# Hybrid streaming encoder step with hierarchical MoE: group 0's expert inputs by one-hot products, and moved splits and first loads around it

## The chip, the core and the metric

The kernel runs on one core of one Trainium2 chip. The metric is the device time of one execution in microseconds, the median of the runs shown. The core has TensorE (PE, with its weight loads shown as PEld), VectorE (DVE), ScalarE (ACT), GpSimd (POOL), SyncE (SP, which here only issues DMAs) and 16 DMA engines. Each engine executes its own instructions in order, and they meet at semaphores.

## What is computed

One layer for two request groups, 256 prompt tokens and 64 sample tokens (320 rows of 1024 values): a mixer of three gated branches, and behind it a mixture of experts. Cut to what matters here:

```python
x = x + mixed @ p["w_out"]
x = x + hier_moe(rmsnorm(x, p["norm_moe_g"]), ...)

def hier_moe(x, w_rg, b_rg, w_re, b_re, w_g, w_u, w_d):
    p_group = softmax(xf @ w_rg + b_rg)
    p_top, grp = top_k(p_group, 1)                      # one of 4 groups
    e_in = (xf @ w_re + b_re) of that group             # 8 experts each
    top_vals, top_idx = top_k(e_in, 2)
    p_exp = softmax(top_vals) * p_top
    for e in range(32):
        hidden = silu(xf @ w_g[e]) * (xf @ w_u[e])      # 1024 -> 256
        y = y + combine[:, e:e + 1] * (hidden @ w_d[e]) # 256 -> 1024
```

Before the mixer's projections the memory rows are projected (w_mem_k, w_mem_v) after an RMSNorm of their own.

## The kernel before

**Precision.** A product of float32 values is made of three fast ones: each operand is split into a rounded high part (ScalarE, a Copy to float32r) and a rest (VectorE, x minus high), and TensorE multiplies high by high, high by rest and rest by high (`PARTS`). A weight unit of 1 MB (128 x 2048) is loaded by SP, its high part made by ScalarE, its rest by VectorE (L988 and L1378 for the dense stage, in a ring of two; L999 and L1387 for the experts, in eight slots). TensorE waits for the rest. Small matrices that need full precision are multiplied as plain float32.

**Order.** `make_steps` writes out a list of steps, and each engine's program walks it and takes from each step its own part. So the place of a step in the list sets the order on all engines. What an engine does besides is tied to a step: ROUND_AT says behind which residual steps (numbered 3 x quarter + place) ScalarE and VectorE split the expert units 0 to 4; LOGITS_AT behind which residual step a pair of logit blocks stands.

**The first microseconds.** SP loads the memory rows and unit 0 in halves, unit 1 and then the rows x, and unit 2 when unit 0's rest is made. At step "memnorm" ScalarE sums the squares of the memory rows (L995), takes the root and then makes unit 1's high part; VectorE computes the scale and then unit 1's rest. POOL loads two narrow slices of w_in (the gate weights, 16 bytes a row) at once.

**The residual stage.** For four quarters of w_out, TensorE makes the residual sums of three row tiles (128, 128 and 64 rows; steps "res": L680 for 128 rows, L606 for the samples, whose two parts lie side by side). VectorE adds them to x_tm (L1643, L1644), ScalarE squares them for the norm (L1200). Behind the first residual of a quarter's successor the previous quarter's columns are transposed (steps "hnT", L816), scaled by the norm's gain into hnT by ScalarE (even blocks, L1203) or VectorE (odd, L1649), and multiplied with the 36 router columns (steps "logits", L621, plain float32, summed over eight blocks). SP writes the finished rows to x_rows in HBM.

**Routing.** VectorE finds each token's group (one-hot `ohg`), TensorE counts each token's rank in its group (L820 to L822) and the totals (L825), VectorE makes `og` (L1347): for each group g a one-hot of tokens by slots (320 x 128). TensorE multiplies og with the token numbers (`slot_tokens`, L841), VectorE turns the result into row numbers (`slot_token`, `slot_out`), POOL gathers the rows of a group's tokens from x_rows (`gather_rows`, L1951), TensorE transposes them (`slot_rows_T`, L861: eight blocks, the columns taken with a step of eight), ScalarE makes the high part with the gain (`slot_x_high`, L1230, eight copies), VectorE the rest (`slot_x_rest`, L1371). Meanwhile VectorE works out the expert weights (from "totals", L1696, to `pone_r`, L1728), which TensorE turns into weights of slots (`slot_weights`, L873). Between these, `keep_busy` (L598) makes products whose results nobody reads.

**Experts.** 32 experts in four groups of eight. In program order on TensorE: gate and up of expert x, first half of the inner dimension (part "A", L896), then part "B", the transposition of the previous expert's hidden rows (L906) between them, and the previous expert's down product (L925). Each part reads one of the 96 units of `STREAM`.

```python
for x in range(E):
    gate_up(lv, x, "A")
    if x in WEIGHTS_AT: slot_weights(lv, WEIGHTS_AT[x])
    if x: hidden_T(lv, x - 1)
    gate_up(lv, x, "B")
    if x: down(lv, x - 1)
    if x in ROWS_AT: slot_rows_T(lv, ROWS_AT[x])
```

Should a group have more than 128 tokens, the whole expert stage is repeated as a further level, from code in a branch; with these inputs it is not.

## Time and profile before

| | |
|---|---|
| runs | 863.65, 863.71, 865.85 us; median 863.71 |
| profiled execution | 862.83 us, span of its instructions 861.0 us |
| TensorE busy | 838.0 us, 97% of the span |
| VectorE, ScalarE, GpSimd busy | 588.8, 471.5, 93.8 us (68%, 55%, 11%) |
| mean granted clock of TensorE | 0.988 of 2.4 GHz |
| HBM read, written | 178.55, 7.93 MB; 217 GB/s over the span |
| chain that ended last | L896 21%, L925 10% of the span, all others 1% or less |

In the rows below times are microseconds from the span's start. A timeline row gives start, duration, engine, line, operation, tiles, count, and in brackets how long the engine stood idle before it and what ended that. The duration of a merged row runs from the first start to the modelled end of the last; the spacing of two rows is read from their starts. Matmuls are pipelined, so a mean duration is longer than the spacing.

### The profile page before, as it was taken

How to read it: one execution, taken by the hardware profiler on the slowest of the kernel's cores; microseconds unless marked ns; L12 is line 12 of the kernel's file. 1: busy time of each engine (PE TensorE's matmuls, PEld its weight loads, DVE VectorE, ACT ScalarE, POOL GpSimd, SP SyncE). 2: the span in 40 equal slices, each digit the busy share in tenths (PEclk: the TensorE clock that was granted, in tenths of full speed). 3: DMA queues.
4: the chain of work that ended last, by engine and by line, in shares of the span. 5: the costliest groups of instructions: out<-in, count | busy, mean ns of one | idle time of the engine just before them, and what ended most of it. 6: DMA issues, size and time to landing. Idle time of an engine off the chain costs nothing. (4 is left out here: it accounts for less than half of the span.)

```text
span 861.0 us, 12938 instructions
## 1 busy us (share of the span) xinstructions
PE 838.0 (97%) x5133; PEld 762.6 (89%) x5133; DVE 588.8 (68%) x824; ACT 471.5 (55%) x639; POOL 93.8 (11%) x153
## 2 busy tenths in 40 slices
PE   6999999999999999999999999899999999999995
PEld 5999999999989998999999999788888888888883
DVE  5665487773445536786656457567889889899893
ACT  4665477753333234454333435545778677767763
POOL 3303001020011011000000000010003111310410
PEclk9999999999999999999999999979999999999998
DMA  8758533334344435345446454469999999999970
GB/s 268 220 169 282 188 111 111 111 123 138 110 135 135 146 123 172 107 139 167 140 147 220 146 197 148 171 223 356 362 341 365 367 388 386 355 375 362 377 270 18
DMA packets 100387, 186.61 MB, mean 217 GB/s; under 512 B 5668, under 2 KB 71488, under 8 KB 100320
## 3 DMA queue, kind: packets, MB, share of 16 engines
q1 hardware_dynamic: 95280, 171.47, 57.9%
q0 software_dynamic: 4240, 12.59, 4.4%
q10 hardware_dynamic: 800, 1.66, 0.5%
q8 instruction: 43, 0.70, 0.3%
q14 instruction: 24, 0.20, 0.1%
HBM read 178.55 MB, written 7.93 MB: 217 GB/s over the span
## 5 line engine op out<-in xcount | busy, mean ns | idle before, releaser
L1378 DVE TENSOR_TENSOR unit_r<-arena,unit_r 128x2048 fp32r<-128x2048 f32 x63 | 144.8, 2299 | 134.9 <-ACT unit_r L988 134.7
L1387 DVE TENSOR_TENSOR w_r<-arena,w_r 128x2048 fp32r<-128x2048 f32 x96 | 216.9, 2286 | 29.2 <-ACT w_r L999 29.2
L592 PE MATMUL pj<-xn_r,unit_r 128*128 128x320 f32 x1536 | 234.0, 311 | 0.0
L592 PEld LDWEIGHTS pj<-xn_r,unit_r 128*128 128x128 f32 x1536 | 225.5, 188 | 3.5 <-issue 3.0
L896 PE MATMUL pj<-w_r,xg 128*128 128x512 f32 x768 | 190.9, 398 | 0.2 <-ACT xg L1230 0.2
L999 ACT ACTIVATE w_r<-arena 128x2048 fp32r<-128x2048 f32 x96 | 180.3, 1909 | 4.4 <-DMA arena<-in_w_exp_up 4.4
L896 PEld LDWEIGHTS pj<-w_r,xg 128*128 128x128 f32 x768 | 141.8, 189 | 30.9 <-issue 0.3
L988 ACT ACTIVATE unit_r<-arena 128x2048 fp32r<-128x2048 f32 x63 | 120.1, 1907 | 24.6 <-PE pj L592 20.0
L925 PE MATMUL pj<-w_r,hidT 128*128 128x512 f32 x384 | 93.4, 392 | 0.6 <-ACT hidT L1243 0.6
L925 PEld LDWEIGHTS pj<-w_r,hidT 128*128 128x128 f32 x384 | 71.8, 188 | 17.1 <-issue 0.8
L592 PE MATMUL pj<-br_r,unit_r 128*128 128x320 f32 x384 | 59.6, 311 | 0.0
L592 PEld LDWEIGHTS pj<-br_r,unit_r 128*128 128x128 f32 x384 | 56.7, 188 | 1.1 <-issue 1.1
L662 PE MATMUL pj<-unit_r,mn_r 128*128 128x256 f32 x384 | 49.9, 291 | 1.8 <-DVE unit_r L1378 1.8
L1243 ACT ACTIVATE hidT<-ms 128x256 fp32r<-128x256 f32 x32 | 12.3, 385 | 71.8 <-PE ms L906 71.8
L662 PEld LDWEIGHTS pj<-unit_r,mn_r 128*128 128x128 f32 x384 | 48.3, 198 | 2.3 <-DVE unit_r L1378 1.8
L592 PE MATMUL pj<-unit_r,xn_r 128*128 128x256 f32 x384 | 48.4, 285 | 0.0
L592 PEld LDWEIGHTS pj<-unit_r,xn_r 128*128 128x128 f32 x384 | 46.7, 191 | 0.4 <-issue 0.3
L592 PE MATMUL pj<-u_r,unit_r 128*128 128x320 f32 x192 | 28.8, 309 | 0.0
L1137 ACT ACTIVATE arena<-pj 128x320 f32<-128x320 f32 x24 | 10.4, 433 | 33.3 <-PE pj L592 33.3
L592 PEld LDWEIGHTS pj<-u_r,unit_r 128*128 128x128 f32 x192 | 28.3, 188 | 0.0
L1394 DVE SCALAR_TENSOR_TENSOR arena<-arena,prT 128x323 f32<-128x323 f32 x48 | 26.9, 561 | 1.7
L680 PE MATMUL pj<-unit_r,mix_r 128*128 128x256 f32 x192 | 24.1, 283 | 0.1
(362 smaller groups left out, 813.3 us busy)
## 6 DMA issues: line engine op xcount, KB each, us to landing
arena<-in_w_in SPq DMA_DIRECT2D x40, 1024.0 KB, 5.2
arena<-in_w_exp_gate SPq DMA_DIRECT2D x64, 512.0 KB, 4.9
arena<-in_w_exp_up SPq DMA_DIRECT2D x64, 512.0 KB, 6.5
arena<-in_w_exp_down SPq DMA_DIRECT2D x64, 512.0 KB, 5.6
arena<-in_w_mem_v SPq DMA_DIRECT2D x4, 1024.0 KB, 6.8
arena<-in_w_br_mem SPq DMA_DIRECT2D x4, 1024.0 KB, 5.1
arena<-in_w_br_mlstm SPq DMA_DIRECT2D x4, 1024.0 KB, 5.1
arena<-in_w_br_gmlp SPq DMA_DIRECT2D x4, 1024.0 KB, 5.1
```

The costliest lines, as they stand in the source:

```text
L592: last = mm(bank_of(s)[0:out_rows, 0:out_cols], l, r, start=k == 0, stop=k == len(pairs) - 1)
L662: last = mm(b[:, 0:256], mn_r[:, p, k, a[1] * 128:a[1] * 128 + 128], w[:, q, k, :], start=k + m == 0, stop=k == KC - 1 and m == 2)
L680: last = mm(b[0:n, 0:256], mix_r[:, p, k, t0:t0 + n], w[:, q, k, :], start=k + m == 0, stop=k == KC - 1 and m == 2)
L896: last = mm(pj[:, x % 2, :].rearrange("p (h n) -> p h n", h=2), xg[g % 2][:, k0 + k, xp, :], w[:, wp, k, :, :], start=k0 + j == 0, stop=k0 ...
L925: last = mm(pj[:, 2 + half, :], hidT[:, x % 2, xp, c, :], w_r[u % NS][:, wp, c * D + half * 512:c * D + half * 512 + 512], start=e == 0 an ...
L988: af(unit_r[n % RING][:, 0, :], ringw[:, n % RING, :], ACT.Copy).then_inc(u_hi, 1)
L999: af(w_r[u % NS][:, 0, :], raw_w[u % NS], ACT.Copy).then_inc(m_hi, 1)
L1137: af(sg[:, k % 2, :], b[:, 0:T], ACT.Sigmoid).then_inc(free, 1)
L1243: af(hidT[:, x % 2, 0, :, :].rearrange("p a b -> p (a b)"), ms[:, x % 2, 0:DE], ACT.Copy).then_inc(m_hth, 1)
L1378: v.tensor_tensor(unit_r[n % RING][:, 1, :], ringw[:, n % RING, :], unit_r[n % RING][:, 0, :], ALU.subtract).then_inc(u_lo, 1)
L1387: v.tensor_tensor(w_r[u % NS][:, 1, :], raw_w[u % NS], w_r[u % NS][:, 0, :], ALU.subtract).then_inc(m_lo, 1)
L1394: ins = v.scalar_tensor_tensor(o, r[:, j:j + CONVW], prT[:, P_CW + 16 * j + c:P_CW + 16 * j + c + 1], o, ALU.mult, ALU.add)
```

## The change

1. *First loads.* POOL issues the two loads of the gate weights only when unit 1 has landed. At "memnorm" ScalarE and VectorE split unit 1 before they work on the memory rows' norm.
2. *Residual stage.* The logits of blocks 2 and 3 stand behind the sample tile of the last quarter, block 4 behind the last residual, block 5 behind the last transpositions. VectorE makes the rests of expert units 2 and 3 behind hnT 3 and hnT 5 instead of behind residual steps.
3. *Group 0's inputs.* TensorE makes the transposed rows of group 0's slots directly, as x_tm (as weights, with a step of eight) times group 0's one-hot, 24 plain float32 products over three row tiles (`first_rows_T`), in place of eight transpositions of gathered rows. The products with token numbers stand behind expert 0's two halves (`first_tokens`), the row numbers are made behind the first hidden rows (`first_index`), so all gathers come later; group 0's gathered rows are used only for its residual sum. The keep-busy products behind "totals" and before the first rows are gone.
4. *Order on ScalarE and VectorE.* ScalarE copies the first four blocks before the router's Exp, the other four behind it, then splits units 6 and 7. VectorE makes the first four rests before its work of "totals", the other four behind pone_r, and the level counters behind those.

The diff, cut to its core:

```diff
@@ -55,13 +55,14 @@
 ROUND_AT = {1: 0, 5: 1, 6: 2, 8: 3, 10: 4}
+REST_AT = {1: 0, 5: 1, 10: 4}
 NO_ROW = 512
...
 QK0, V0, O0, I0, F0, U0, GV0, MQ0, GATE0 = 0, 2048, 3072, 4096, 4100, 4104, 5128, 6152, 7176
-LOGITS_AT = {(2, 0): 1, (2, 2): 2, (3, 1): 3}
+LOGITS_AT = {(2, 0): (0, 1), (3, 0): (2, 3), (3, 2): (4,)}
 RES_ORDER = ((0, 1, 2), (0, 1, 2), (0, 1, 2), (2, 0, 1))
@@ -188,12 +189,12 @@
                     step("hnT", c, ring="hx", eng="AD"[c % 2])
-            if (u, j) in LOGITS_AT:
-                for c in (2 * LOGITS_AT[u, j] - 2, 2 * LOGITS_AT[u, j] - 1):
-                    step("logits", c, ring=None, eng=None)
+            for c in LOGITS_AT.get((u, j), ()):
+                step("logits", c, ring=None, eng=None)
     step("moe_var", ring=None, eng=None)
...
     step("hnT", 7, ring="hx", eng="D")
+    step("logits", 5, ring=None, eng=None)
     step("moe_norm", ring=None, eng=None)
@@ -824,16 +825,12 @@
                 last.then_inc(ready[s["ring"]], 1)
-                if kind == "totals":
-                    keep_busy(2)
             def slot_tokens(lv):
-                until(pe, m_xgl, 2 * G * lv)
-                if isinstance(lv, int):
-                    pe.wait_ge(s_tokid, 1)
+                pe.wait_ge(m_xgl, 2 * G * lv)
                 for g in range(G):
@@ -842,6 +839,23 @@
                         last.then_inc(m_slot, 1)
+            def first_tokens(g0, g1):
+                for g in range(g0, g1):
+                    for i in range(3):
+                        last = mm(ms[:, 3, 2 * g:2 * g + 2], og[:, i, g, :], tokid[:, i, :], start=i == 0, stop=i == 2)
+                last.then_inc(m_slot, 1)
+            def first_rows_T():
+                pe.wait_ge(m_onehot, 1)
+                for half in range(2):
+                    for k in range(4):
+                        for i, (t0, n) in enumerate(TILES):
+                            cols_of = x_tm[0:n, i, :].rearrange("t (p k) -> t k p", k=KC)
+                            last = mm(pj[:, 2 + half, k * 128:(k + 1) * 128], cols_of[:, 4 * half + k, :], og[0:n, i, 0, :].bitcast(FP32), start=i == 0, stop=i == 2)
+                    last.then_inc(m_rowT, 1)
             def slot_rows_T(lv, g):
@@ -851,6 +865,7 @@
                         pe.wait_ge(freed["hx", e], _seen["hx", e])
+                    pe.wait_ge(m_outrow, 2 * lv + 2)
                 if g >= 2:
@@ -880,7 +895,7 @@
                     k0 = 4
-                if x == 0 and part == "A":
+                if x == 0 and part == "A" and not isinstance(lv, int):
                     pe.wait_ge(m_index, 2 * lv + 2)
@@ -929,18 +944,25 @@
             def level(lv):
-                slot_tokens(lv)
                 if isinstance(lv, int):
-                    keep_busy(9)
-                slot_rows_T(lv, 0)
+                    first_rows_T()
+                else:
+                    slot_tokens(lv)
+                    slot_rows_T(lv, 0)
                 for x in range(E):
...
                         slot_weights(lv, WEIGHTS_AT[x])
+                    if x == 0 and isinstance(lv, int):
+                        pe.wait_ge(s_tokid, 1)
+                        pe.wait_ge(m_onehot, G)
+                        first_tokens(0, 2)
                     if x:
...
                     gate_up(lv, x, "B")
+                    if x == 0 and isinstance(lv, int):
+                        first_tokens(2, G)
                     if x:
@@ -1015,12 +1044,12 @@
                 if kind == "memnorm":
+                    unit_first_part(1)
                     for i in range(2):
...
                     af(sd[:, 3:5], var[:, 3:5], ACT.Sqrt).then_inc(s_sd, 1)
-                    unit_first_part(1)
                 elif kind == "xnorm":
@@ -1206,9 +1235,12 @@
                 elif kind == "lgt":
                     unit_high(0, 5)
-                    unit_high(0, 6)
+                    act.wait_ge(s_gpk, 16)
+                    slot_x_high(0, 0, 0)
                     act.wait_ge(s_lgx, 1)
                     af(expo.rearrange("p a b -> p (a b)"), expo.rearrange("p a b -> p (a b)"), ACT.Exp).then_inc(s_lge, 1)
+                    slot_x_high(0, 0, 1)
+                    unit_high(0, 6)
                     unit_high(0, 7)
...
                 if kind == "unit_split":
@@ -1407,11 +1436,11 @@
                 if kind == "memnorm":
+                    unit_second_part(1)
                     dve.wait_ge(s_ss, 2)
...
                     refine(1, 3, 5, s_rsm)
-                    unit_second_part(1)
                 elif kind == "xnorm":
@@ -1642,11 +1671,13 @@
                     v.tensor_tensor(x_, x_, b[0:n, 0:256], ALU.add).then_inc(free, 1)
-                    if 3 * u + s["place"] in ROUND_AT:
-                        unit_rest(0, ROUND_AT[3 * u + s["place"]])
+                    if 3 * u + s["place"] in REST_AT:
+                        unit_rest(0, REST_AT[3 * u + s["place"]])
                 elif kind == "hnT" and a[0] % 2:
...
                     v.tensor_scalar(hnT[:, c, :], b[:, 0:T], prT[:, P_MOE + c:P_MOE + c + 1], None, ALU.mult).then_inc(free, 1)
+                    if c in (3, 5):
+                        unit_rest(0, 2 if c == 3 else 3)
                 elif kind == "moe_var":
@@ -1676,9 +1707,7 @@
                     dve.wait_ge(*done("ranks"))
-                    token_onehots(0, 2)
-                    slot_index(0, 0)
-                    token_onehots(2, G)
+                    token_onehots(0, G)
                     v.tensor_tensor(expo[:, :, 0:G], lg[:, :, 0:G], gmax[:, :, 0:1].to_broadcast([128, 3, G]), ALU.subtract)
@@ -1690,16 +1719,11 @@
                     v.tensor_tensor(expo[:, :, G:G + 1], emax[:, :, 1:2], emax[:, :, 0:1], ALU.subtract).then_inc(s_lgx, 1)
-                    slot_index(0, 1)
-                    output_rows()
+                    dve.wait_ge(s_gpk, 16)
+                    slot_x_rest(0, 0, 0)
                 elif kind == "totals":
...
                     v.tensor_copy(cnt[:, 3:4], cnt[:, 0:1]).then_inc(free, 1)
-                    link(v.tensor_scalar(cnt[:, 1:2], cnt[:, 0:1], SLOTS + 0.5, None, ALU.is_ge))
-                    for lv in range(2, LEVELS):
-                        link(v.tensor_scalar(cnt[:, 2:3], cnt[:, 0:1], lv * SLOTS + 0.5, None, ALU.is_ge))
-                        link(v.tensor_tensor(cnt[:, 1:2], cnt[:, 1:2], cnt[:, 2:3], ALU.add))
-                    v.tensor_copy(more[:, :], cnt[:, 1:2]).then_inc(s_more, 1)
                     for i in range(3):
@@ -1726,6 +1750,12 @@
                     v.tensor_tensor(pone_r[:, 1, :, :], weights, pone_r[:, 0, :, :], ALU.subtract).then_inc(s_pone, 1)
+                    slot_x_rest(0, 0, 1)
+                    link(v.tensor_scalar(cnt[:, 1:2], cnt[:, 0:1], SLOTS + 0.5, None, ALU.is_ge))
+                    for lv in range(2, LEVELS):
+                        link(v.tensor_scalar(cnt[:, 2:3], cnt[:, 0:1], lv * SLOTS + 0.5, None, ALU.is_ge))
+                        link(v.tensor_tensor(cnt[:, 1:2], cnt[:, 1:2], cnt[:, 2:3], ALU.add))
+                    v.tensor_copy(more[:, :], cnt[:, 1:2]).then_inc(s_more, 1)
                 if kind == "unit_split":
@@ -1754,19 +1784,25 @@
             def y_add(lv, g, half):
...
                     dve.wait_ge(m_yhalf, G * lv + g + 1)
+                    if g == 0 and isinstance(lv, int):
+                        dve.wait_ge(m_row[0], 16)
                 else:
...
             def level(lv):
-                slot_x_rest(lv, 0)
+                if not isinstance(lv, int):
+                    for half in range(2):
+                        slot_x_rest(lv, 0, half)
                 for u in (range(5, 6) if isinstance(lv, int) else range(2, 5)):
...
                     hidden(lv, x - 1)
+                    if x == 1 and isinstance(lv, int):
+                        first_index()
                     if x > 1 and x - 1 in WEIGHTS_AT:
@@ -1855,6 +1892,7 @@
             pool.wait_ge(s_wifz, 1)
+            pool.wait_ge(unit_full[1], 16)
             for c0, col in ((0, I0), (32, F0)):
...
```

TensorE in the last quarter of the residual stage, before. The first L606 group is the sample tile of quarter 2, the second that of quarter 3 (`pair_mix`, 16 products); L621 are logits (three tiles a block, `wr` the router columns); L816 hnT 4 and 5; L680 a tile of 128 rows.

```order
L606 MATMUL pj<-unit_r_53,pair_mix 128x256 x16
L621 MATMUL ms<-wr,arena 128x36 x2
L621 MATMUL ms<-wr,arena 64x36
L621 MATMUL ms<-wr,arena 128x36 x2
L621 MATMUL ms<-wr,arena 64x36
L606 MATMUL pj<-unit_r_54,pair_mix 128x256 x16
L816 MATMUL ms<-ident,arena 128x128 x2
L816 MATMUL ms<-ident,arena 128x64
L816 MATMUL ms<-ident,arena 128x128 x2
L816 MATMUL ms<-ident,arena 128x64
L680 MATMUL pj<-unit_r_54,mix_r 128x256 x24
```

The same place with the change (L607, L622, L817, L681 are the same lines, shifted).

```order
L607 MATMUL pj<-unit_r_53,pair_mix 128x256 x16
L607 MATMUL pj<-unit_r_54,pair_mix 128x256 x16
L817 MATMUL ms<-ident,arena 128x128 x2
L817 MATMUL ms<-ident,arena 128x64
L817 MATMUL ms<-ident,arena 128x128 x2
L817 MATMUL ms<-ident,arena 128x64
L622 MATMUL ms<-wr,arena 128x36 x2
L622 MATMUL ms<-wr,arena 64x36
L622 MATMUL ms<-wr,arena 128x36 x2
L622 MATMUL ms<-wr,arena 64x36
L681 MATMUL pj<-unit_r_54,mix_r 128x256 x48
```

The logits of blocks 2 and 3 stood between the two sample groups; they stand now behind the transpositions, and the sample groups follow each other.

VectorE there, before: L1644 and L1643 add a residual tile (64 rows: samples), L1649 is hnT 3, L1387 the rest of an expert unit (`w_r_62` unit 2, `w_r_63` unit 3).

```order
L1644 TENSOR_TENSOR arena<-arena,pj 128x256
L1387 TENSOR_TENSOR w_r_62<-arena,w_r_62 128x2048
L1658 MEMSET arena 64x36
L1659 MEMSET arena 128x15
L1661 CAST tokid<-tokf 128x6
L1644 TENSOR_TENSOR arena<-arena,pj 128x256
L1649 TENSOR_SCALAR arena<-ms,prT 128x320
L1643 TENSOR_TENSOR arena<-arena,pj 64x256
L1644 TENSOR_TENSOR arena<-arena,pj 64x256
L1387 TENSOR_TENSOR w_r_63<-arena,w_r_63 128x2048
L1643 TENSOR_TENSOR arena<-arena,pj 64x256
```

With the change (L1673, L1672, L1678, L1416):

```order
L1673 TENSOR_TENSOR arena<-arena,pj 128x256
L1689 MEMSET arena 64x36
L1690 MEMSET arena 128x15
L1692 CAST tokid<-tokf 128x6
L1673 TENSOR_TENSOR arena<-arena,pj 128x256
L1678 TENSOR_SCALAR arena<-ms,prT 128x320
L1416 TENSOR_TENSOR w_r_62<-arena,w_r_62 128x2048
L1672 TENSOR_TENSOR arena<-arena,pj 64x256
L1673 TENSOR_TENSOR arena<-arena,pj 64x256
L1672 TENSOR_TENSOR arena<-arena,pj 64x256
L1673 TENSOR_TENSOR arena<-arena,pj 64x256
L1678 TENSOR_SCALAR arena<-ms,prT 128x320
```

Unit 2's rest stood ahead of the addition of the second tile and stands behind hnT 3; unit 3's stood ahead of the sample tile of quarter 3 and now comes behind hnT 5.

TensorE from the totals (L825) to expert 0's second half, before. L598 are keep-busy products, L841 products with token numbers, L861 the transpositions, L896 gate and up, L873 slot weights.

```order
L825 MATMUL ms<-arena,ones 128x4 x3
L598 MATMUL pj<-ident 128x128 x2
L841 MATMUL ms<-tokid,og 128x2 x3
L841 MATMUL pj<-tokid,og 128x2 x9
L598 MATMUL pj<-ident 128x128 x9
L861 MATMUL pj<-ident,arena 128x128 x8
L896 MATMUL pj<-w_r_60,xg_69 128x512 x12
L873 MATMUL ms<-pone_r,og 128x20 x3
L896 MATMUL pj<-w_r_61,xg_69 128x512 x12
```

With the change (totals L826, L856 the new products, L911 gate and up, L888 slot weights, L846 token numbers):

```order
L826 MATMUL ms<-arena,ones 128x4 x3
L856 MATMUL pj<-og,arena 128x128 x24
L911 MATMUL pj<-w_r_60,xg_69 128x512 x12
L888 MATMUL ms<-pone_r,og 128x20 x3
L846 MATMUL ms<-tokid,og 128x2 x6
L911 MATMUL pj<-w_r_61,xg_69 128x512 x12
L846 MATMUL ms<-tokid,og 128x2 x6
L911 MATMUL pj<-w_r_62,xg_69 128x512 x12
```

Two groups of keep-busy products, the token products and the transpositions between the totals and expert 0 are replaced by 24 products of the residual rows with `og`; the token products stand on both sides of expert 0's second half.

## Rows read from the trace of the kernel before

**Rows 1.** Groups of TensorE's instructions; columns: busy us, mean ns, idle before.

```profile
L896 PE MATMUL pj<-w_r,xg 128*128 128x512 f32 x768 | 190.9, 398 | 0.2 <-ACT xg L1230 0.2
...
L598 PE MATMUL pj<-ident 128*128 128x128 f32 x30 | 6.2, 379 | 0.0
```

**Rows 2.** Timeline of the first 60 us, SP, ScalarE and TensorE.

```profile
3.71 0.66 SPq L557 DMA_DIRECT2D arena<-in_w_mem_k  x1
...
15.48 1.90 ACT L988 ACTIVATE unit_r<-arena 128x2048 fp32r<-128x2048 f32 x1
...
19.76 3.13 PE L662 MATMUL pj<-unit_r,mn_r 128*128 128x256 f32 x24 [1.57 <-DVE unit_r L1378]
...
21.91 1.92 ACT L988 ACTIVATE unit_r<-arena 128x2048 fp32r<-128x2048 f32 x1 [3.21 <-DMA arena<-in_w_mem_k]
...
26.30 3.11 PE L662 MATMUL pj<-unit_r,mn_r 128*128 128x256 f32 x24 [0.24 <-DVE unit_r L1378]
```

**Rows 3.** DMA issues from 3.7 to 4.1 us; columns: count, KB each, us to landing.

```profile
arena<-in_w_mem_k SPq DMA_DIRECT2D x1, 1024.0 KB, 11.0
```

**Rows 4.** Timeline of the residual stage, TensorE and one row of VectorE.

```profile
538.13 2.28 DVE L1387 TENSOR_TENSOR w_r<-arena,w_r 128x2048 fp32r<-128x2048 f32 x1
...
538.25 2.18 PE L606 MATMUL pj<-unit_r,pair_mix 128*128 128x256 f32 x16
...
542.22 1.97 PE L621 MATMUL ms<-wr,arena 128*128 128x36 f32 x12 [1.80 <-ACT arena L1203]
...
544.12 3.33 PE L606 MATMUL pj<-unit_r,pair_mix 128*128 128x256 f32 x16
...
558.04 1.67 PE L621 MATMUL ms<-wr,arena 128*128 128x36 f32 x12 [0.70 <-ACT arena L1203]
...
559.64 1.40 PE L598 MATMUL pj<-ident 128*128 128x128 f32 x8
```

**Rows 5.** Windows of TensorE; columns: us, busy (instructions), granted clock, DMA share, GB/s.

```profile
543.00:544.00 1.00, 1.00 (x8) 0.67 0.99 393
546.00:547.00 1.00, 1.00 (x7) 0.63 0.00 0
560.00:561.00 1.00, 1.00 (x8) 0.70 0.89 332
570.00:571.00 1.00, 1.00 (x8) 0.68 0.66 217
```

**Rows 6.** Timeline of routing and the first experts, TensorE.

```profile
562.86 1.42 PE L825 MATMUL ms<-arena,ones 128*128 128x4 f32 x6
...
564.14 1.20 PE L598 MATMUL pj<-ident 128*128 128x128 f32 x4
...
567.79 3.61 PE L598 MATMUL pj<-ident 128*128 128x128 f32 x18
...
571.24 1.13 PE L861 MATMUL pj<-ident,arena 128*128 128x128 f32 x8
...
572.53 3.13 PE L896 MATMUL pj<-w_r,xg 128*128 128x512 f32 x12 [0.16 <-ACT xg L1230]
...
575.49 0.40 PE L873 MATMUL ms<-pone_r,og 128*128 128x20 f32 x3
...
575.74 5.83 PE L896 MATMUL pj<-w_r,xg 128*128 128x512 f32 x24
...
581.41 0.38 PE L906 MATMUL ms<-ident,arena 128*128 128x128 f32 x2
```

**Rows 7.** Timeline of routing, ScalarE and VectorE.

```profile
568.30 0.14 DVE L1696 TENSOR_REDUCE cnt<-ms 1x1 f32<-1x4 f32 x1
...
572.02 2.17 ACT L1230 ACTIVATE xg<-pj,gpk 128x128 fp32r<-128x128 f32 x8 [0.27 <-PE pj L861]
...
573.04 0.28 DVE L1728 TENSOR_TENSOR pone_r<-arena,pone_r 128x120 fp32r<-128x120 f32 x1
...
573.27 2.16 DVE L1371 SCALAR_TENSOR_TENSOR xg<-pj,gpk,xg 128x128 fp32r<-128x128 f32 x8
```

More of the change, by code:

```diff
@@ L992, in first_unit_high, with slot_x_high @@
                 af(unit_r[0][:, 0, cs], ringw[:, 0, cs], ACT.Copy).then_inc(signal, 1)
+            def slot_x_high(lv, g, half):
+                banks = pj if g == 0 else ms
+                act.wait_ge(m_rowT, 2 * (G * lv + g) + half + 1)
+                for j in range(4):
+                    k = 4 * half + j
+                    af(xg[g % 2][:, k, 0, :], banks[:, 2 + half, j * SLOTS:(j + 1) * SLOTS], ACT.Copy, scale=gpk[:, k:k + 1]).then_inc(m_xgh, 1)
             def memory_squares(i):
@@ L1271, in level @@
                     if x - 1 in ROWS_AT:
-                        slot_x_high(lv, ROWS_AT[x - 1])
+                        g_next = ROWS_AT[x - 1]
+                        if g_next >= 2:
+                            act.wait_ge(m_used, NU * lv + AT[EPG * (g_next - 1) - 1, "B"] + 1)
+                        for half in range(2):
+                            slot_x_high(lv, g_next, half)
                     hidden_high(lv, x - 1)
@@ L1762, in level @@
             def level(lv):
-                slot_x_rest(lv, 0)
+                if not isinstance(lv, int):
+                    for half in range(2):
+                        slot_x_rest(lv, 0, half)
                 for u in (range(5, 6) if isinstance(lv, int) else range(2, 5)):
@@ L1783, in level @@
                     if x - 1 in ROWS_AT:
-                        slot_x_rest(lv, ROWS_AT[x - 1])
+                        for half in range(2):
+                            slot_x_rest(lv, ROWS_AT[x - 1], half)
                     hidden_rest(lv, x - 1)
```

35 lines of the change are left out of this document (13 added, 22 removed).

## The prediction, made before the run

> **What bounds the kernel now.** I read the grouped instruction lines of TensorE first. The reader is to see there that in the expert stage 768 products of w_r and xg wait 0.2 us in all [rows 1]: from the first expert on TensorE sets the pace, and every microsecond by which the experts start earlier is one by which the kernel ends earlier. The timelines then show where TensorE waits for others, and that is at two places, the ones that the change touches.
>
> At the start [rows 2] TensorE stands 1.57 us before unit 1 (at 19.76) for VectorE's split, which follows ScalarE's first part at 15.48, and 0.24 us before unit 2 (at 26.30). In the residual and router stage [rows 4] it stands 1.80 us before the logits of blocks 2 and 3 and 0.70 us before those of 6 and 7. The windows of the granted clock [rows 5] show the rest: the clock falls from 2.4 to 1.2 GHz at 543.3, after the first of these waits and products of 36 columns, is back at 546.7, falls again at 560.4 after the second, and is back at 570.6. Both returns come about 2.7 us after a dense run of products began (544.12 [rows 4], 567.79 [rows 6]).
>
> I measure everything to one point, the transposition of expert 0's hidden rows (L906, 581.41 [rows 6]): what follows it is the same in both kernels and is TensorE's own work.
>
> **Start: 0.2 us.** Unit 1 was issued at 3.71 and took 11.0 us to land [rows 2, 3], so it lies there at 14.7, and ScalarE began on it at 15.48 because of two sums of squares. Moved ahead of them it gains 0.8 us for unit 1, and the squares still fit before unit 2. But unit 2 is then what TensorE waits for: ScalarE stood 3.21 us for its data until 21.91 [rows 2], and the split and the products follow from there. The wait before 19.76 shrinks and the one before 26.30 grows by as much. Unit 2 comes earlier only if the gate weights, whose loads POOL now issues behind unit 1, had been in its way; they are 32 KB, but in small pieces. Bounds: nothing, and both waits, 1.8 us. I take 0.2, nearest to the row in which data, not an engine, is late.
>
> **Residual stage: 4.1 us.** The logits of 2 and 3 move behind the sample rows of the last quarter and its two transpositions; block 4 goes to the end of the residuals, 5 behind the last transpositions. VectorE's rest of unit 2, 2.28 us at 538.13 [rows 4], moves behind the third and fourth transposed block, so the additions and hnT 3 come some 2 us earlier; the rest of unit 3 moves likewise. Both units are read by TensorE only in expert 1, behind expert 0's two halves, from about 578 on (575.74 + 2.96 [rows 6]), so their cover is ample. TensorE from 538.25: two sample groups of 2.1 (the row's 2.18 less its tail), 0.3 of waiting for VectorE's addition, transpositions 1.1, two logit blocks 1.5, two dense groups of 24 in 5.9 together, logits 0.8, transpositions 1.15, three logit blocks of 0.8: 17.3 us, so the logits end at 555.55 and not at 559.64 [rows 4]. Read by what vanishes: 1.8 and 0.7 of waiting, 1.15 of the sample group at the low clock (3.33 against 2.18), 0.4 in other waits and slower logits. Bounds 3.2 (if the clock is low in the last logits already) and 4.4. The copy of x_rows and the loads of units 6 and 7 are issued earlier with it; ScalarE reaches unit 6 only after group 0's eight copies, but TensorE reads it in expert 2, behind the point that I measure to, so nobody waits.
>
> **Routing: 1.1 us given back.** From the end of the logits to the first keep-busy product after the totals are 4.5 us (559.64 to 564.14 [rows 4, 6]); group 0's one-hot is there by then. Removed on this path: 22 keep-busy instructions, 12 token products, the gather and eight transpositions. Added are 24 fp32 products of 128 columns, 48 instructions, since an fp32 product takes two (12 logit instructions for six products). Their price is in no row as such. At the high clock 12 logit instructions with the same alternation of 128- and 64-row tiles start 1.60 us before what follows, 0.133 each [rows 4]; at the low one six take 1.28 us, 0.213 each [rows 6]. So all 48 cost between 6.4 and 10.2 us. The clock is most likely low when they begin, since the 8 us before hold logits, short products and waits as before 560.4. I take it back to 2.4 GHz after 2.8 us, as both returns in rows 5: 13 instructions at 0.213, 35 at 0.133, 7.45 us.
>
> Now both paths, counted from 560.05 (555.55 + 4.5). TensorE: products to 567.5, the first gate and up half 2.96 us (572.53 to 575.49 [rows 6]), to 570.5. The router weights: the first 24 instructions end at 564.3 (2.8 + 11 x 0.133); ScalarE's four copies start 0.27 later and take half of 2.17; VectorE's four rests 0.1 later half of 2.16; then VectorE's chain from the totals to pone_r, from 568.30 to 573.32, less four one-element counters now moved behind, 0.15 each by their like at 568.30, 4.4 [rows 7]. Sum 7.0, so pone_r is ready at 571.3. This is the **new wait**: the chain was done 2.2 us before TensorE asked (573.32 against 575.49) and now comes 0.85 late, because the four rests stand ahead of it on VectorE and they wait for ScalarE. From 571.35: slot weights 0.25, six token products, the second half 2.96, six token products, expert 1's first half 2.8. The token products I take at 0.55 for six (three router products of rows 6 start 0.25 before the next; all at the low clock they would be 1.3). That gives 578.45 against 581.41, **2.95 us** earlier; 4.1 won before, 1.1 given back.
>
> The work behind keeps its cover. After pone_r VectorE does xg's second half (1.1), the counters (0.6), the rest of unit 5 (2.3) and the comb copies (0.4), 4.4 us; only then can the first activation and hidden product run, and TensorE asks for them 7.1 us after pone_r. The slot numbers and the gathers come some 9 us later; TensorE needs their rows first in expert 5 and VectorE at the end of group 0. SP's next load (unit 8) waits for the first half's end, which is earlier than before.
>
> **Sum.** 2.9 + 0.2 = 3.1 us. The profiled execution spans 861.0 and took 862.83; it becomes 857.9 and 859.7. The median of the three runs, 863.71, lies 0.9 over the profiled one, so I forecast **860.6**. A measurement of this kernel can tell about 0.3% (2.6 us) from no change.
>
> **Rivals.**
> 1. *The products run slowly throughout*: the clock stays low to their end, 10.2 us. Half at 565.15, pone_r at 572.15, first gate half ended at 573.2, the point at 580.4: 1.0 gained and 0.2 at the start, 862.5. For: the clock stayed low for 10 us (560.4 to 570.6) in spite of the keep-busy and token products in it. Against: two returns after 2.7 us. 0.15.
> 2. *The residual stage keeps its wait*: what held hnT was VectorE's queue, and the later place lets another of its tasks (unit 3's rest, the additions) stand in the way for the same 1.8 us. 862.4. Against: with the rests moved VectorE is free when the samples' products end. 0.10.
> 3. *The start pays in full*: the gate weights were the delay, unit 2 lands up to 1.6 us sooner and both waits go. Then 3.1 + 1.6, 859.0. For: ScalarE, VectorE and TensorE are all free to use it. Against: the data before unit 2 are the same in sum. 0.15.
> 4. *Slower: dear products.* The residual rows are read as weights with a step of eight elements. If such a load does not hide behind the product before it, an instruction costs the 0.379 us that a keep-busy product has by itself [rows 1]: 18.2 us, the point at 588.4, 7.0 later, less 0.2: 870.5. It decides from 11.25 us on, 0.234 an instruction. Against: eight transpositions with the same step are done in 1.13 us [rows 6], 0.14 each, tail included. 0.05.
>
> On rival 4 the Trainium skill has a rule: *SBUF — State Buffer*, section "Door 1: The DMA port swizzle", in the note on cachelines, says that a read with a step over four fp32 elements pays for every new line, and this step is eight. By that rule the products would go the way of rival 4; the transposition row does not agree with it, and I leave the sum as it is.
>
> The forecast itself has 0.55, with a range of its own from 859.5 to 861.9. **Faster** by over 0.3% (under 861.1): rival 3 and four fifths of the forecast's own, 0.59. **Within**: rivals 1 and 2 and the rest, 0.36. **Slower**: rival 4, 0.05. The range reaches from rival 3 with the clock high in all products (858.0) to rival 1 with the residual stage at its lower bound of 3.2 (863.3).
>
> **What would show it.** The logits should follow without a wait before 543; their last instruction should end near 555.5 and the clock not fall before about 553. The products are 48 instructions starting near 560, in 6.4 to 10.2 us; in that time the clock rises. Then a wait of about 0.9 us before the slot weights, released by VectorE's pone_r, and the L906 of expert 0 near 578.3. At the start the wait before unit 1 falls to about 0.8 and that before unit 2 grows to about 1. I am wrong if an instruction of the products costs over 0.2 us at the high clock, if the wait for pone_r is over 2 us, or if TensorE still waits a microsecond or more among the residual groups.

## Result and the profile after

The changed kernel takes 871.33 us (median of four runs, 869.92 to 872.14) against 864.35 (863.65 to 865.85) for the kernel before: ratio 1.0079, 95% interval 1.0063 to 1.0094, **slower** by 7.0 us (0.8%). The forecast was 860.6 with a range from 858.0 to 863.3. The profiled execution spans 868.2 us and took 869.92.

Timeline of TensorE in the changed kernel, the start and the stretch from the last residual quarter to the point (rows give start, duration, line, operation):

```profile
core 0 of [0], span 868.2 us
...
10.44 10.89 PE L663 MATMUL pj<-unit_r,mn_r 128*128 128x256 f32 x72
...
26.14 1.07 PE L663 MATMUL pj<-unit_r,mn_r 128*128 128x256 f32 x7 [1.64 <-DVE unit_r L1407]
...
538.07 4.10 PE L607 MATMUL pj<-unit_r,pair_mix 128*128 128x256 f32 x32
...
552.37 2.93 PE L622 MATMUL ms<-wr,arena 128*128 128x36 f32 x18
555.23 2.08 PE L599 MATMUL pj<-ident 128*128 128x128 f32 x8
...
559.73 16.24 PE L856 MATMUL pj<-og,arena 128*128 128x128 f32 x48
575.90 5.45 PE L911 MATMUL pj<-w_r,xg 128*128 128x512 f32 x12
581.19 0.40 PE L888 MATMUL ms<-pone_r,og 128*128 128x20 f32 x3
...
588.44 0.38 PE L921 MATMUL ms<-ident,arena 128*128 128x128 f32 x2
```

Read beside [rows 2, 4, 6]: no wait stands in the residual stage any more, and the logits end at 555.23 where they ended at 559.64. The products (L856, 48 instructions) begin at 559.73 and last until the first gate half starts at 575.90: 16.17 us. That half takes 5.29 us to 581.19 and not 2.96. Then no wait for pone_r, and the point, the transposition of expert 0 (now L921), stands at 588.44 and not at 581.41: 7.03 later. The spans differ by 7.2, so nothing that matters happens behind it.

The windows of the changed kernel (columns as in [rows 5]; the number after POOL's busy time is the granted clock, 0.50 for 1.2 GHz and 1.00 for 2.4):

```profile
553.00:554.00 1.00, 1.00 (x9) 0.87 (x8) 0.86 (x6) 1.00 (x1) 0.00 (x0) 0.94 0.98 234
554.00:555.00 1.00, 1.00 (x5) 0.93 (x6) 0.00 (x1) 0.65 (x1) 0.00 (x0) 0.50 1.05 279
565.00:566.00 1.00, 1.00 (x4) 0.78 (x4) 0.00 (x0) 0.00 (x0) 0.00 (x0) 0.50 0.00 0
580.00:581.00 1.00, 1.00 (x4) 0.81 (x3) 1.00 (x1) 0.98 (x2) 0.00 (x0) 0.50 0.00 0
581.00:582.00 1.00, 1.00 (x10) 0.90 (x9) 0.43 (x3) 1.00 (x1) 0.00 (x0) 0.91 0.00 0
```

The clock fell at 554 and stayed at 1.2 GHz for 27 us, through all the products and the first gate half. The weight loads show something else. These are PEld rows (start, duration, line; the bracket is the time in which the loader stood), first the last twelve loads of the logits of the kernel before, then the first of the products of the changed one:

```profile
558.03 1.56 PEld L621 LDWEIGHTS ms<-wr,arena 128*128 128x128 f32 x12 [0.94 <-ACT arena L1203]
```
```profile
559.67 1.05 PEld L856 LDWEIGHTS pj<-og,arena 128*128 128x128 f32 x4
560.94 0.55 PEld L856 LDWEIGHTS pj<-og,arena 64*128 64x128 f32 x2 [0.22 <-issue]
561.71 0.55 PEld L856 LDWEIGHTS pj<-og,arena 128*128 128x128 f32 x2 [0.22 <-issue]
```

In the logits of before the 12 loads follow without a gap that the view shows. In the products the loader stands 0.22 us at each change between tiles 128 rows high (128\*128) and 64 rows high (64\*128). The starts of the single instructions in the trace repeat with each block of six: 0.24 us apart within a height, 0.37 to 0.40 for each of the two instructions behind a change, so two short and four long ones: 0.24 + 0.24 + 0.37 + 0.40 + 0.37 + 0.40 = 2.02, times eight 16.2.

### The profile page after: what moved, and what is told of

Same layout as the page of the kernel before. It is cut to its first block and busy times, and to the rows that moved or that the text cites. A ratio compares the mean times of both kernels' runs of the same rounds, so it can differ in the third digit from the quotient of the medians.

```text
span 868.2 us, 12975 instructions
## 1 busy us (share of the span) xinstructions
PE 848.7 (98%) x5151; PEld 770.1 (89%) x5151; DVE 588.6 (68%) x822; ACT 471.7 (54%) x639; POOL 95.1 (11%) x153
## 5 line engine op out<-in xcount | busy, mean ns | idle before, releaser
L1416 DVE TENSOR_TENSOR w_r<-arena,w_r 128x2048 fp32r<-128x2048 f32 x96 | 216.9, 2285 | 27.7 <-ACT w_r L1028 27.7
L911 PE MATMUL pj<-w_r,xg 128*128 128x512 f32 x768 | 193.4, 402 | 0.0
L911 PEld LDWEIGHTS pj<-w_r,xg 128*128 128x128 f32 x768 | 143.4, 191 | 31.1 <-issue 0.2
L681 PE MATMUL pj<-unit_r,mix_r 128*128 128x256 f32 x192 | 23.9, 283 | 0.1
```

Of the source, the lines that this page charges most:

```text
L681: last = mm(b[0:n, 0:256], mix_r[:, p, k, t0:t0 + n], w[:, q, k, :], start=k + m == 0, stop=k == KC - 1 and m == 2)
L911: last = mm(pj[:, x % 2, :].rearrange("p (h n) -> p h n", h=2), xg[g % 2][:, k0 + k, xp, :], w[:, wp, k, :, :], start=k0 + j == 0, stop=k0 ...
L1416: v.tensor_tensor(w_r[u % NS][:, 1, :], raw_w[u % NS], w_r[u % NS][:, 0, :], ALU.subtract).then_inc(m_lo, 1)
```

## Experiments

The kernel before took 864.4 to 864.8 us (medians of 16 to 34 runs) beside each group of runs, so times can be compared through the ratios.

**1. The residual part alone** on the kernel before: LOGITS_AT, the place of block 5, and the rests of units 2 and 3 as in the change, nothing else.

> The kernel before with the residual stage of the change alone (logits and rests moved), start and routing as before. Both theories of the products say the same here: the logits end near 555.3 us instead of 559.6, the routing of before takes its 21.8 us from there, and the kernel ends about 4 us earlier than before, near 860 us. If the residual stage were what cost the time, it would end near 871.

859.94 us, ratio 0.9937 (0.9908 to 0.9965). The logits end at 554.74, the point stands at 577.41 (timeline of TensorE):

```profile
554.74 2.06 PE L599 MATMUL pj<-ident 128*128 128x128 f32 x8
...
559.25 1.20 PE L599 MATMUL pj<-ident 128*128 128x128 f32 x4
...
566.87 1.81 PE L862 MATMUL pj<-ident,arena 128*128 128x128 f32 x8
568.54 3.11 PE L897 MATMUL pj<-w_r,xg 128*128 128x512 f32 x12
...
577.41 0.38 PE L907 MATMUL ms<-ident,arena 128*128 128x128 f32 x2
```

The forecast's largest term holds at the point: 4.0 us, 4.1 forecast. It is made of two parts. The logits end 4.9 us earlier, 0.6 before the expected 555.3; from there to the point it takes 22.7 us and not 21.8 as before, and the clock is low for 13.7 us there (554.79 to 568.45) and not for 10.2 (560.4 to 570.6). The loss of the whole change is in what remains.

**2 to 5. The two things peculiar to the products.** A square of runs: the third tile with 64 rows or, its missing rows set to zero, with 128; the weights as every eighth column, or as 128 neighbouring ones (which gives group 0's inputs in another order of columns, so that part of the output differs). A further run keeps the 64-row tile and the step and only changes the order, with the 64-row products last in each half. The diff is cut, and shows the two edits of the square in one.

```diff
-    mm(..., cols_of[0:n, 4 * half + k], og[0:n, i, 0, :], ...)
+    mm(..., cols_of[:, 4 * half + k], og[:, i, 0, :], ...)    # full height
+link(v.memset(x_tm[64:128, 2, :], 0.0))                      # full height, at the start
+pe.wait_ge(s_tokid, 1)                                       # full height, before the products
...
+    mm(..., x_tm[0:n, i, c * 128:(c + 1) * 128], ...)         # or: neighbouring columns
```

> The change with the third tile of the new products made 128 rows high (its upper 64 rows are zero in x_tm, cleared at the start, and in the one-hot). Height theory: the change from 128 to 64 rows and back leaves the weight load bare, so without it the 48 instructions start 0.24 us apart at the low clock as neighbours of one height do now, 11.3 us, or 7 to 9 us if the denser run brings the clock back; the kernel is 4 to 9 us faster than the change. Step theory (weights read with a step of eight elements are dear): nothing changes, 16.2 us.

> The change with the weights of the new products read as 128 neighbouring columns instead of with a step of eight; this permutes the inner dimension against the expert weights, so the experts' inputs are others. Step theory: the instructions start 0.213 us apart at the low clock, 10.2 us or less, and the kernel is 6 us or more faster than the change. Height theory: 16.2 us as in the change, 0.338 each, and the same time.

> The change with the order of the new products turned within each half: four blocks of the first tile, four of the second, then four of the 64-row tile, so that the height changes twice per half instead of eight times. Height theory: 48 x 0.24 us and four changes of some 0.3 us, 12 to 13 us at the low clock, less if the clock returns; the kernel is 3 to 8 us faster than the change. Step theory: 16.2 us, the same time.

> The change with both suspected prices taken out of the 48 product instructions: the third tile read with 128 rows (the added rows zero), and the weights of each product as 128 neighbouring columns, not every eighth (so group 0's inputs come out in another order of columns: that part of the output differs). Theory (two prices add: bare loads at a change of row height, and a load of about 0.238 us for weights with a step): 0.213 us an instruction while the clock is low, 0.11 to 0.13 once it is high, which comes after some 3 to 5 us; 7 to 8 us in all against 16.2 in the change and 11.45 with full height alone. Point (expert 0's hidden transposition) near 578.5, time 860.5 to 862. Rival (the step of the weights costs nothing, and the 0.239 of the full-height run is the price of any fp32 product of 128 columns): 11.4 us again, 864.5.

```profile
561.16 11.69 PE L857 MATMUL pj<-og,arena 128*128 128x128 f32 x48
572.61 3.03 PE L912 MATMUL pj<-w_r,xg 128*128 128x512 f32 x12
575.47 0.40 PE L889 MATMUL ms<-pone_r,og 128*128 128x20 f32 x3
...
582.73 0.38 PE L922 MATMUL ms<-ident,arena 128*128 128x128 f32 x2
```
```profile
558.59 15.04 PE L856 MATMUL pj<-og,arena 128*128 128x128 f32 x48
573.55 4.88 PE L911 MATMUL pj<-w_r,xg 128*128 128x512 f32 x12
...
585.51 0.38 PE L921 MATMUL ms<-ident,arena 128*128 128x128 f32 x2
```
```profile
558.92 8.16 PE L857 MATMUL pj<-og,arena 128*128 128x128 f32 x48
566.84 3.03 PE L912 MATMUL pj<-w_r,xg 128*128 128x512 f32 x12
571.26 0.50 PE L889 MATMUL ms<-pone_r,og 128*128 128x20 f32 x3 [1.39 <-DVE pone_r L1754]
...
578.61 0.38 PE L922 MATMUL ms<-ident,arena 128*128 128x128 f32 x2
```

These are TensorE's timelines, from above: full height with every eighth column; 64 rows with neighbouring columns; both. From the first product to the point:

| | third tile 64 rows | third tile 128 rows |
|---|---|---|
| every eighth column | 28.71 us (the change) | 21.57 us, 864.5 (ratio 0.9997, 0.997 to 1.0024) |
| neighbouring columns | 26.92 us, 866.92 (one run only) | 19.69 us, 861.8 (0.9959, 0.994 to 0.9977) |

Up to the point the height costs 7.1 and 7.2, the step 1.8 and 1.9. That the two seem to add so well is chance. In the 48 instructions alone (16.17, 14.96, 11.45 and 7.92 us for the four) the step costs 1.2 with 64 rows, where the clock stays low, and 3.5 at full height, where it comes back; and of these 3.5 the wait for pone_r, 1.39 us, takes back the most. With both gone 19.7 us remain, near the 18.4 that the forecast had between the same places (560.05 to 578.45). Of the 1.3 left over, 0.5 is the longer wait for pone_r (1.39 where 0.9 stood in the sum), 0.5 is in the products, and 0.3 behind them.

How each works is read from the starts of the single instructions. With both gone they stand 0.213 apart at the low clock and 0.112 at the high one. With the step alone (full height) they stand 0.239 apart at the low clock and the same 0.239 when it is high. The weight loads show it too, here at the high clock, first with the step, then without (count, busy us, mean ns of one):

```profile
L857 PEld LDWEIGHTS pj<-og,arena 128*128 128x128 f32 x28 | 6.8, 337 | 0.0
L857 PEld LDWEIGHTS pj<-og,arena 128*128 128x128 f32 x21 | 2.4, 192 | 0.0
```

At the low clock they are 335 and 333 ns: the load with the step does not follow the clock. With the height alone the instructions stand 0.213 apart within a height and 0.35 to 0.375 behind a change. The run with the 64-row tile last in each half, where the height changes three times and not 15, confirms it: products 12.60 us, and long spacings only at the three changes and, as in all these runs, behind the first of the 48 instructions; 866.06 us (1.0025, 1.0001 to 1.0048).

Against what was expected: full height gave 11.45 us (11.3 expected at the low clock), but stayed there when the clock came back, where 7 to 9 were expected. Neighbouring columns alone met neither theory, 14.96 us against 10.2 or 16.2: each theory had one of two prices. The other two came out as expected (12.60 of 12 to 13, 7.92 of 7 to 8 us, the point at 578.61 of 578.5).

**6. The clock.** In the windows of the run with full height it came back inside the products (0.78 is the window in which it rose), in the change it did not:

```profile
565.00:566.00 1.00, 1.00 (x7) 1.00 (x5) 0.00 (x0) 0.00 (x0) 0.00 (x0) 0.78 0.00 0
566.00:567.00 1.00, 1.00 (x6) 1.00 (x5) 0.00 (x0) 0.00 (x0) 0.00 (x0) 1.00 0.00 0
```

To see which is cause and which effect, 28 dense keep-busy instructions were put ahead of the products:

```diff
 pe.wait_ge(m_onehot, 1)
+keep_busy(14)
 for half in range(2):
```

> The change with 28 dense keep-busy instructions put between the wait for the one-hot and the 48 product instructions, so that the clock is back at 2.4 GHz before the products begin. They cost 4.5 us themselves (13 at 0.213, 15 at 0.112). Theory A (the low clock is a consequence: the products are bound by the weight load and the bare changes of height, and keep or lose the clock by themselves): at the high clock same-height instructions still 0.239, changes of height 0.30 to 0.35, products 14 to 15.5 us; the first expert half 2.96 and not 5.45 if the clock holds; time 868.5 to 872, so little changed. Theory B (the price of the products is the clock's): products 8 us, time 864. If the clock falls again inside the 48, the run of products itself is what lets it fall.

Timeline and windows of this run:

```profile
560.81 6.28 PE L599 MATMUL pj<-ident 128*128 128x128 f32 x28
566.92 15.70 PE L857 MATMUL pj<-og,arena 128*128 128x128 f32 x48
582.55 5.25 PE L912 MATMUL pj<-w_r,xg 128*128 128x512 f32 x12
```
```profile
566.00:567.00 1.00, 1.00 (x7) 1.00 (x6) 0.00 (x0) 0.00 (x0) 0.00 (x0) 0.54 0.00 0
567.00:568.00 1.00, 1.00 (x6) 0.88 (x5) 0.00 (x0) 0.00 (x0) 0.00 (x0) 1.00 0.00 0
570.00:571.00 1.00, 1.00 (x4) 0.88 (x5) 0.00 (x0) 0.00 (x0) 0.00 (x0) 0.66 0.00 0
571.00:572.00 1.00, 1.00 (x4) 0.78 (x4) 0.00 (x0) 0.00 (x0) 0.00 (x0) 0.50 0.00 0
```

The clock was back when the products began, and fell again at 570.3, in their midst; they took 15.63 us and the first gate half 5.09. 876.67 us (1.013, 1.0079 to 1.0181): the 6.1 us of keep-busy were paid for almost nothing. Theory A holds in its mechanism, but not in its time (868.5 to 872): the keep-busy instructions ran at the low clock to their end, 6.1 and not 4.5 us, and the clock did not hold. At the high clock, before it fell, the spacings were 0.239 within a height and 0.33 to 0.34 behind a change, so a block of six takes 1.8 us and not 2.0. By these spacings, as an estimate, the high clock throughout would save 1.7 of 16.2 us in these products; what it costs beside that to lose it is the gate half behind them, 2.3 us. So the alternating products are slow by themselves, and in them the clock neither returned nor held. With only three changes it did not return in them either (low until 574.3); with neighbouring columns and 15 changes it was low until 577.6. So it goes with the 64-row tile and not with the step; whether the changes or the 64-row instructions do it these runs do not tell apart.

**7. The start part.** Alone on the kernel before, taken out of the change, and added to the residual part:

> The kernel before with the start part alone (unit 1's splits ahead of the memory squares, gate-weight loads behind unit 1). Forecast: 0.2 us gained (0 to 1.6). Theory from the profiles so far: the two waits of 1.57 and 0.24 us become one of about 1.6 us before unit 2, nothing is gained, and where the clock falls in or behind that one wait 1 to 1.5 us are lost: a ratio of 1.000 to 1.002 to the kernel before.

> The change without its start part. Theory: the whole loss is in the products, so it stands where the change does, 870 to 871.5; if the start's single wait costs clock in some executions, it is up to 1 us faster than the change. Rival (the start part is what turned the forecast around): near 861 to 864.

> The kernel before with the start part and the residual part, without the new products. Theory: the residual part's gain of 4 us stands, the start adds nothing: 859.5 to 861.5, point at 577.2 to 577.8. Rival (start pays as forecast or in full): 858 to 859.5.

> The change with full height of the third tile and without the start part. The products cost 11.4 to 11.5 us (0.239 each at either clock). Theory (the start part joins two waits into one and is worth nothing or a loss): 0 to 1.4 us faster than full height with the start part (864.5), 863 to 864.5. Rival (the start part pays): 864.7 or more.

| | with the start part | without |
|---|---|---|
| kernel before | 865.27 (1.0003, 0.9985 to 1.0021) | 864.5 |
| and the residual part | 860.84 (0.9947, 0.993 to 0.9965) | 859.94 (0.9937, 0.9908 to 0.9965) |
| the change | 871.33 (1.0079, 1.0063 to 1.0094) | 869.72 (1.005, 1.003 to 1.007) |
| the change, full height | 864.5 (0.9997, 0.997 to 1.0024) | 863.47 (0.9976, 0.9952 to 1.0) |

Each pair lies on the same side, by 0.0003 to 0.0029 of the time (0.3 to 2.5 us), though the intervals of each pair overlap: the part gains nothing and probably costs about a microsecond; its exact size stays open. In the profiles it does what the forecast said, and more: the wait before unit 1 goes altogether, and the one before unit 2 becomes 1.0 to 2.7 us. With the longest ones the clock fell, as here in the run with start and residual part (timeline, then window):

```profile
26.81 3.42 PE L663 MATMUL pj<-unit_r,mn_r 128*128 128x256 f32 x17 [2.68 <-DVE unit_r L1379]
```
```profile
28.00:29.00 1.00, 1.00 (x7) 1.00 (x7) 0.75 (x5) 1.00 (x4) 0.00 (x0) 0.50 0.89 273
```

In three of the eight profiles with the start part the clock fell there (waits of 2.37, 2.50 and 2.68 us), in five it did not (1.04 to 1.97). Of the six profiles without the part one shows it low in this stretch, behind a wait of 1.73 us before unit 1; three others waited 1.89, 2.16 and 2.17 us there and kept it. So the length of the wait alone does not decide. In the run with start and residual part, whose profile has such a fall, the point stood at 579.57, where 577.2 to 577.8 were expected. Its median met the expectation, and so did those of the other three, but for 869.72 where 870 to 871.5 were expected.

**8. A form of the change without its two prices.** No start part, full height, and every block of columns a neighbouring one, in all groups, with the expert weights and the gain loaded to match (pieces of 1 KB and not 4). Then, on top of it, the router's work moved ahead of the first half's copies and rests:

```diff
-src = I[name][0, x].rearrange("(p k) n -> p k n", k=KC)...
+src = I[name][0, x].rearrange("(k p) n -> p k n", k=KC)...
```
```diff
 unit_high(0, 5)
-slot_x_high(0, 0, 0)
 act.wait_ge(s_lgx, 1)
 af(expo..., ACT.Exp)
+slot_x_high(0, 0, 0)
 slot_x_high(0, 0, 1)
...
-slot_x_rest(0, 0, 0)
 ... totals to pone_r ...
+slot_x_rest(0, 0, 0)
 slot_x_rest(0, 0, 1)
```

> A form of the change with both prices removed and the reference's result: no start part, third tile 128 rows high, and each of the eight blocks of group inputs is 128 neighbouring columns in all groups, the expert gate and up weights and the gain loaded to match (pieces of 1 KB, not 4 KB, in those loads). Products 8 us as in the run with full height and plain columns, point near 578.6, a wait for pone_r of 1.4 us. If the smaller pieces of the weight loads stay hidden: 860.5 to 862, about with the residual part alone (859.9). Rival (the loads with smaller pieces are late in the expert stage, where 360 to 396 GB/s are moved): waits on data before splits, 865 to 900.

> The kernel of the run with neighbouring columns everywhere, with the router's exponential on ScalarE and VectorE's chain from the totals to pone_r moved ahead of the four copies and the four rests of group 0's first half. There TensorE waited 1.22 us for pone_r (ready at 570.60), while VectorE stood 3.15 us before the rests at 565.13. Theory (the forecast's new wait is real and comes from the place of the rests in VectorE's queue): pone_r ready at about 566.4, during the products; the wait goes, the point falls from 578.0 to 576.8, time 860.0 to 860.6, ratio 0.9935 to 0.995. Rival (the first gate half then waits for the late rests, from 566.4 to 567.5): the wait moves before the ninth product of that half and half of the gain stays away, point at 577.4.

TensorE's timelines of the two:

```profile
559.44 7.23 PE L857 MATMUL pj<-og,arena 128*128 128x128 f32 x48 [0.28 <-DVE og L1374]
566.42 3.02 PE L912 MATMUL pj<-w_r,xg 128*128 128x512 f32 x12
570.66 0.50 PE L889 MATMUL ms<-pone_r,og 128*128 128x20 f32 x3 [1.22 <-DVE pone_r L1754]
...
578.00 0.38 PE L922 MATMUL ms<-ident,arena 128*128 128x128 f32 x2
```
```profile
559.41 8.17 PE L857 MATMUL pj<-og,arena 128*128 128x128 f32 x48
567.33 3.03 PE L912 MATMUL pj<-w_r,xg 128*128 128x512 f32 x12
570.20 0.40 PE L889 MATMUL ms<-pone_r,og 128*128 128x20 f32 x3
...
577.45 0.38 PE L922 MATMUL ms<-ident,arena 128*128 128x128 f32 x2
```

861.46 us (0.9957, 0.9935 to 0.9979) and 860.51 (0.9948, 0.9928 to 0.9968). The loads of smaller pieces took 7.9 and not 4.9 us from issue to landing (w_exp_gate), and TensorE did not wait for them: from the point to the end both take 279.6 to 279.7 us, the kernel before 279.6. In the second, pone_r was ready at 566.17, during the products, and the wait of 1.22 us is gone; of it 0.94 was taken back by the products, since the clock had fallen at 554.6 already and not at 560.7. The gate half did not wait for the late rests (2.87 us). So the point of the rival, 577.4, was met, but not for its reason. Both come near the residual part alone (859.94), neither beats it: from the first product to the point they need 18.6 and 18.0 us, and the gather with its keep-busy products 18.2 (559.25 to 577.41), or 17.3 in the kernel before (564.14 to 581.41). The lowest median of all the runs is that of the residual part alone; against the last run of 8 the intervals overlap.

## Why the prediction was wrong

**What held.** TensorE bounds the experts, and the point decides. The forecast put the break-even of the products at 11.25 us; with 11.45 us, the run with full height, the time was that of the kernel before (0.9997). The residual stage: 4.1 forecast, 4.0 at the point by itself (run 1, 4.9 less 0.9), and in the change the logits end at 555.23 against 555.55. The products begin at 559.73, forecast 560.05. The start did not hold: 0.2 forecast, nothing or a loss measured, at or under the lower bound; the fall of the clock behind the joined wait was not in them.

**What failed is the price of the 48 instructions**, 7.45 us in the sum with bounds of 6.4 and 10.2; it was 16.17. The sign that I had named came true, an instruction over 0.2 us at the high clock: 0.239. The bounds came from the logits "with the same alternation of 128- and 64-row tiles". They have none. The forms of the instructions say so, first the last logits of the kernel before (min/median/max ns, first and last start), then the products of the changed one (busy us, mean ns):

```profile
L621 PE MATMUL ms<-wr,arena x12: 226/279/300, 558.0 to 559.5; 128*128 128x36 f32 x8, 128*64 128x36 f32 x4
```
```profile
L856 PE MATMUL pj<-og,arena 128*128 128x128 f32 x32 | 10.5, 483 | 0.0
L856 PE MATMUL pj<-og,arena 64*128 64x128 f32 x16 | 6.7, 523 | 0.0
```

In the logits the tile's 64 is the number of weight columns (128\*64, all 128 rows in use), in the products it is the number of rows (64\*128). A tile of 64 tokens is the one when tokens are columns and the other when tokens are summed over. The upper bound was therefore no bound. What the alternation in the logits does cost is small and already in the 0.133: their instructions start 0.21 and 0.16 us apart at a change between 128 and 64 columns, 0.11 to 0.13 within 128 columns, and 0.08 within 64.

The 8.7 us between 7.45 and 16.17 are:
- the clock, low throughout: 48 x 0.213 = 10.2, so 2.8. This was rival 1, to which I gave 0.15. It goes with the 64-row tile, the third term: with full height and the same step the clock came back inside the products, with 64 rows and no step it did not.
- the step of eight at the low clock, 16.17 against 14.96 (neighbouring columns): 1.2. At full height, where the clock comes back, it is 3.5 of 11.45 (against both gone). This was rival 4's mechanism, but not its price: 0.239 an instruction at either clock and not 0.379.
- the change of height, 16.17 against 11.45 (full height): 4.7. No rival named it.

Behind them, 2.3 us in the first gate half, at the low clock (5.29 against 2.96). The new wait for pone_r did not appear (0.9 less than forecast), since ScalarE and VectorE had the products' 16 us to finish: pone_r was ready at 574.65. With 0.3 less for the earlier begin and 0.2 more for the rest: 8.7 + 2.3 - 0.9 - 0.3 + 0.2 = 10.0, from 578.45 to 588.44. The point of rival 4, 588.4, was met by luck, by a sum with other terms. From the forecast's 860.6 to 871.33 it is 10.7: 10.0 at the point, 0.2 that the start was to give, and 0.5 because the median lies 1.4 over the profiled execution and not 0.9.

**The wait was real.** Where the products cost what the forecast took, it stood where it was put: 1.39 us in the run with both prices gone (pone_r ready at 571.20, forecast 571.3), and the point there at 578.61 against 578.45. Moving four rests behind the chain removed it (the last run of 8). So the path behind the products was priced within a microsecond, and the products, with the clock that they left to the gate half, turned the sign. That the products themselves came so near in that run, 7.92 us for 7.45, is partly luck: the clock was back after 5.4 us and not 2.8, and the instructions then cost 0.112 and not 0.133.

**The evidence against rival 4** was the eight transpositions with the same step, 1.13 us [rows 6]. It is true and does not carry over: they are one instruction each, and follow 0.113 apart. On the rule that I cited and did not follow (the Trainium skill, *SBUF — State Buffer*, section "Door 1: The DMA port swizzle", the note on cachelines): for the products the trace agrees, 0.239 against 0.112 us at 2.4 GHz and against 0.213 at 1.2; for the transpositions it shows no price. On the height the Trainium skill has a rule too, in *TensorEngine Tiling (Array Packing)*, section "Key Properties": changing the tiling mode drains TensorE. The runs agree with it, if 64 rows under 128 count as another mode: 0.35 to 0.40 us behind each change where 0.213 to 0.239 stand within a height. That the loader stood for a drain is not shown otherwise, and the change between 128 and 64 columns in the logits costs far less.

## What to carry over

Price a new product from a row with the same form, rows times columns of the weights and their step, not from one with the same tile sizes: "64" in the rows and "64" in the columns cost differently. Where a sum over tokens has a short last tile, pad it with zeros to full height or put all short tiles together (11.45 and 12.60 us here for 16.17). And before an indirect path (gather, transposition) is replaced by products, compare both ends on the critical path: here even the best form of the products only equalled the gather, 18.0 against 18.2 us, and the forecast itself had them 1.1 us dearer.

## What the runs showed of the hardware

- A change between weights of 128 and of 64 rows costs 0.14 to 0.16 us for each of the two instructions behind it at 1.2 GHz (0.35 to 0.375 against 0.213), in either direction, and 0.1 at 2.4 GHz (0.33 to 0.34 against 0.239, with a step).
- Between weights of 128 and of 64 columns, all 128 rows in use, the change is cheap: six float32 instructions of the logits, four with 128 and two with 64 columns, take 0.80 us at 2.4 GHz.
- A float32 product of 128 columns whose weights are taken with a step of eight elements costs 0.239 us an instruction at 1.2 and at 2.4 GHz. With neighbouring columns it is 0.213 and 0.112. At 1.2 GHz it is 0.213 with 4 moving columns as well (six instructions in 1.28 us, from 558.45 to 559.73 in the change).
- TensorE was never idle in the change's 48 instructions by the profile's busy column, yet the clock stayed at 1.2 GHz through them, and in the run with keep-busy products it fell from 2.4 in their midst. In all five runs with the third tile at full height it rose within the products; in the runs with 64 rows it was low at their end.
